# Four slots and a new load order for the raw w_down tiles of the sample's down projection

## The chip, the cores and the metric

One NeuronCore of a Trainium2 chip runs the whole program. The metric is the device time of one execution, in microseconds (us); a profiled execution also has a span, from the first to the last instruction in the trace.

## The reference, cut to what matters

One layer of a hybrid encoder on 1024 prompt frames and 32 sample frames, in float32: RMSNorm, a combined input projection, windowed attention beside a gated mixing group, an output projection with residual, and then the part that this case is about:

```python
def swiglu(h, w_gate, w_up, w_down):
    return (jax.nn.silu(h @ w_gate) * (h @ w_up)) @ w_down      # D_MODEL 1024, D_FF 2816

yp = yp + swiglu(rms_norm(yp, g_ffn[l]), ...)   # 1024 rows
ys = ys + swiglu(rms_norm(ys, g_ffn[l]), ...)   # 32 rows
y = rms_norm(y, g_final)
```

## The kernel before, in words

All matrix products of the prompt are float32 made of three passes over a high and a low part (fp32r), so every operand is first split: ScalarE (ACT) writes the high part, VectorE (DVE) the low part. The FFN is done with a seven-product (Strassen-like) scheme. This case is about the last phase, the down projection (PE from 819 us to the end).

**Stages and groups.** The down projection of the prompt has 7 stages (n = 0 to 6, one product each) of 6 groups (g = 0 to 5). Form k = 6n + g is the pair of operands of group g in stage n: a w part and an x part, 512 KB each (256 KB where g = 5, which has one pair of d_ff tiles in place of two). PE does, for each of 4 token tiles t, 6 matmuls of 128x512 for a group (3 where g = 5), so 24 (12) for a group. The products of stages 0 and 1 are summed in the same four PSUM banks.

**What makes a form.** SP issues all the loads, in the order of its program (`load_w`, `load_x`): load k waits until form k - 3 is split, as there are 3 staging buffers. ACT casts (`down_weight_hi`, `act_hi`, lines 1686 and 1700), DVE subtracts (line 1746), into a ring of 8 forms; form k waits for group k - 8.

**Between stages.** In the first stages, after the casts of the next stage's six forms ACT copies the four finished PSUM tiles out (`copy_out`, line 1716); at n = 0 that is the copy into `down_u`, which bumps `u_copied`. PE's stage 1 adds on to the same banks and waits for that copy tile by tile (`bank_free`). In ACT's program this stands as

```python
for n in range(STAGES - 1):
    for g in range(GROUPS_A_FORM):
        form_hi(n + 1, g)
    if n in (0, 1, 3):
        for t in range(TILES):
            copy_out(n, t)
```

and in PE's `bank_free`, called for every tile of a stage's first group:

```python
elif p == P2:                       # stage 1
    pe.wait_ge(u_copied, t + 1)
```

**The sample.** The 32 sample rows are multiplied with w_down as it is, in plain float32: 22 raw tiles r (11 for each half of d_model, 512 KB each), loaded by `load_raw` (line 806) into slots in the unused `y_acc_odd`. `down_sample(r)` (line 1364) does two matmuls of a tile. `SAMPLE_TURNS` says after which groups (n, g) PE does how many of them; "turn (0,5)" is that after group 5 of stage 0. Tile r goes to slot r % 2 and waits until tile r - 2 has been used (`raw_used`).

**SP's order around it.** Loads 0 to 5, raw tiles 0 and 1, the last stores of the hidden values, loads 6 and 7, `store_sums` (the last 1 MB of `act_sums` to DRAM), then a wait until those have landed (line 838), the sample's residual (line 840), and loads 8, 9, 10, 11. Raw tiles 2 and 3 come behind load 11, tiles 4 and 5 in front of load 14, 6 and 7 in front of load 15, 8 and 9 in front of load 16, 10 in front of load 17.

Of the kernel before, what the change touches and what calls it, by code (L numbers as in the profile page):

```python
# [30 lines left out]
CHUNKS = STEPS // 2  # L31
# [7 lines left out]
P1, P6, P5, P7, P2, P3, P4 = range(PRODUCTS)  # L39
# [29 lines left out]

SAMPLE_BANK = DOWN_B[3]  # L70
QUARTERS = [slice(DEC * x, DEC * x + DEC) for x in range(4)]
SAMPLE_TURNS = {(0, 3): 2, (0, 5): 2, (1, 0): 2, (1, 1): 2, (1, 2): 2, (1, 3): 1,
                (3, 0): 2, (3, 2): 2, (3, 4): 2, (4, 0): 2, (4, 2): 2, (4, 3): 1}
RAW_SLOTS = 2


def raws_before(n, g):

    return sum(c for at, c in SAMPLE_TURNS.items() if at < (n, g))

# [136 lines left out]
def product_count(s, p, j):  # L217

    if isinstance(s, int) and s == 0:
        return PRODUCTS * j + p + 1  # L220
    return 2 * PRODUCTS * s + (2 * p + j + 1)
# [12 lines left out]
def build(nc, a, o):  # L234
# [3 lines left out]
    with ExitStack() as ctx:  # L238
# [3 lines left out]
        def sem(name):  # L242
            return ctx.enter_context(nc.semaphore(name))
# [67 lines left out]
        def place(name, shape, at, dt=F32):  # L311
            return nc.alloc_sbuf_tensor_at(name, shape, dt, offset=at)
# [34 lines left out]
                     place("sample_in_odd", [P, CHUNKS, DEC], h_at + 43008)]  # L347
        y_even = place("y_acc_even", [P, TILES, D], work_at + 40960)
        y_odd = place("y_acc_odd", [P, TILES, D], work_at)
        raw = [y_odd[:, 2 * x:2 * x + 2, 0:512] for x in range(RAW_SLOTS)]  # L350
        y_sample = place("y_acc_sample", [DEC, D], work_at + 57344)
        du = place("down_u", [P, TILES, 512], trans_at)
        resid = [place("resid_0", [P, D], wsp_at), place("resid_1", [P, D], stage_at + 8192)]
# [104 lines left out]
        product_done = sem("product_done")  # L458
# [16 lines left out]
        wd_in_landed = [sem(f"wd_in_landed{x}") for x in range(STAGED_FORMS)]  # L475
        xd_in_landed = [sem(f"xd_in_landed{x}") for x in range(STAGED_FORMS)]
        sample_landed = [sem(f"sample_landed{x}") for x in range(2)]
        raw_landed = [sem(f"raw_landed{x}") for x in range(RAW_SLOTS)]
        raw_used = sem("raw_used")
        sample_back = sem("sample_back")  # L480
        resid_landed = [sem(f"resid_landed{x}") for x in range(2)]
# [84 lines left out]
        def _(sp):  # L566
# [4 lines left out]
            w_down = a["w_down"][0].rearrange("(f p) c -> p f c", p=P)  # L571
# [73 lines left out]
            for n in range(4, UNIT_FFN):  # L645
# [8 lines left out]
                if n in g_state_after:  # L654

                    g = g_state_after[n]
# [61 lines left out]
            def store_sums(c):  # L718

                for j in range(2):  # L720
                    sp.wait_ge(act_sums_ready, 6 * c + (3 * j + 3))
                    sp.dma_start(act_rows[:, bass.ds(STAGES * c + A_S2, 4), 2 * P * j:2 * P * j + 2 * P],
                                 act_sum[j][:, :, :]).then_inc(act_sums_out[j], 16)
# [15 lines left out]
            def store_piece(c, x):  # L739

                sp.wait_ge(t_ready, 4 * PIECES * c + (4 * x + 4))
                sp.dma_start(t_rows[:, bass.ds(c, 1), :, P * x:P * x + P].rearrange("p c x t -> p (c x) t"),
                             t_out[x % 2][:, :, :]).then_inc(t_stored[x % 2], 16)
# [27 lines left out]
            def load_w(k):  # L771

                n, g = divmod(k, GROUPS_A_FORM)
                c0, pairs = GROUP * g, GROUP_PAIRS[g]
                if k >= STAGED_FORMS:
                    sp.wait_ge(w_dn_lo, k - STAGED_FORMS + 1)
                else:
                    sp.wait_ge(product_done, product_count(last, [P1, P1, P5][k], 1))
                if n in PLAIN_OF:
                    e, h = PLAIN_OF[n]  # L780
                    src = w_down[:, 2 * c0 + e:2 * (c0 + pairs):2, 512 * h:512 * h + 512]
                else:
                    src = t_pairs[:, T_OF[n], c0:c0 + pairs, :]
                dst = wd_in[k % STAGED_FORMS][:, 0:pairs, :]
                sp.dma_start(dst, src).then_inc(wd_in_landed[k % STAGED_FORMS], 16)

            def load_x(k):

                m, g = divmod(k, GROUPS_A_FORM)
                c0, pairs = GROUP * g, GROUP_PAIRS[g]  # L790
                if k >= STAGED_FORMS:
                    sp.wait_ge(x_dn_lo, k - STAGED_FORMS + 1)
                else:
                    sp.wait_ge(product_done, product_count(last, [P6, P6, P5][k], 1))
                form = A_OF[STAGE_PRODUCT[m]]
                dst = xd_in[k % STAGED_FORMS][:, 0:pairs, :]
                sp.dma_start(dst, act_pairs[:, form, c0:c0 + pairs, :]).then_inc(xd_in_landed[k % STAGED_FORMS], 16)

            def load_raw(r):

                h, c = divmod(r, CHUNKS)
                if r >= RAW_SLOTS:
                    sp.wait_ge(raw_used, r - RAW_SLOTS + 1)
                else:
                    sp.wait_ge(product_done, product_count(last, P4, 0))
                sp.dma_start(raw[r % RAW_SLOTS], w_down[:, 2 * c:2 * c + 2, 512 * h:512 * h + 512]
                             ).then_inc(raw_landed[r % RAW_SLOTS], 16)

            def load_resid(k):
                if k >= 2:  # L810
                    sp.wait_ge(resid_used, k - 1)
                i = [0, 2, 4, 6, 1, 3, 5, 7][k]
                sp.dma_start(resid[k % 2][:, :], y_scratch[row_tokens(i), :]).then_inc(resid_landed[k % 2], 16)

            last = STEPS - 1
# [8 lines left out]
                    sp.wait_ge(product_done, product_count(last, P7, 1))  # L824
                    sp.dma_start(sample_in[0][:, :, :], sample_scratch.ap()[:, 0, :, :]).then_inc(sample_landed[0], 16)
            store_piece(CHUNKS - 1, 3)
            for r in range(RAW_SLOTS):
                load_raw(r)
            store_step(CHUNKS - 1, 1)
            for j in range(2):  # L830
# [2 lines left out]
            for k in (GROUPS_A_FORM, GROUPS_A_FORM + 1):  # L833
                load_w(k)
                load_x(k)
            store_sums(CHUNKS - 1)
            for j in range(2):
                sp.wait_ge(act_sums_out[j], 16 * CHUNKS)
# [1 line left out]
            sp.dma_start(y_sample[:, :], y_scratch[row_tokens(SAMPLE), :]).then_inc(sample_back, 16)  # L840
            for n in range(1, STAGES):
                for g in range(2 if n == 1 else 0, GROUPS_A_FORM):
                    if g >= 2:
                        for r in range(max(RAW_SLOTS, raws_before(n - 1, g - 2)), raws_before(n - 1, g - 1)):
                            load_raw(r)
                    load_w(GROUPS_A_FORM * n + g)
                    load_x(GROUPS_A_FORM * n + g)
                for r in range(raws_before(n - 1, 4), raws_before(n, 0)):
                    load_raw(r)
                if n in (2, 4, 5):  # L850
                    for k in ((0, 1) if n == 2 else (2, 3) if n == 4 else (4, 5)):
                        load_resid(k)
# [173 lines left out]
        def _(pe):  # L1026
# [326 lines left out]
            def down_sample(r):  # L1353

                h, c = divmod(r, CHUNKS)
                if r == 0:
                    pe.wait_ge(c12_ready, 2 * STEPS)
                    for x in range(2):
                        pe.wait_ge(sample_landed[x], 16)
                if r == CHUNKS:  # L1360
                    pe.wait_ge(u2_down, TILES)
                pe.wait_ge(raw_landed[r % RAW_SLOTS], 16 * (r // RAW_SLOTS + 1))
                for e in range(2):
                    last = mm(ps[QUARTERS[(2 * c + e) % 4], SAMPLE_BANK, :], sample_in[e][:, c, :],  # L1364
                              raw[r % RAW_SLOTS][:, e, :], start=c < 2, stop=c >= CHUNKS - 2)
                last.then_inc(raw_used, 1)

            for n in range(STAGES - 1):
                for g in range(GROUPS_A_FORM):
                    for t in range(TILES):  # L1370
                        down_group(n, g, t)
                    for r in range(raws_before(n, g), raws_before(n, g + 1)):
                        down_sample(r)
# [883 lines left out]
```

## Time and profile before

| what | value |
|---|---|
| three runs | 1063.82, 1065.97, 1066.91 us; median 1065.97 |
| the profiled execution's own time | 1065.66 us |
| its span | 1063.9 us (1.8 us of its time lie outside the span) |
| PE matmul busy | 1022.2 us, 96% of the span |
| DVE, ACT, POOL busy | 625.9, 391.0, 385.3 us |
| DMA in the stretch 841 to 859 us | 308 GB/s, engines 0.87 busy |

The engines: PE is the matmul engine, PEld its weight loads, SPq the queue of DMA issues. A timeline row has the start, the duration, the engine, the line, the operation and the tiles it writes and reads, and in square brackets the idle time before it and what ended that. For a DMA issue the duration is that of the issue, not of the transfer. Consecutive rows of the same kind can be merged: x4 is four of them.

### The profile page before, as it was taken

The page shows a single profiled execution, that of the slowest core. Times are in us where ns is not written, and L with a number is a line of the kernel's source. Part 1 is how long each engine was busy: PE and PEld are TensorE (multiplying, and loading weights), DVE is VectorE, ACT ScalarE, POOL GpSimd, SP SyncE. Part 2 cuts the span into 40 slices and gives each one's busy share as a digit, 9 for nine tenths or more (in the row PEclk, how much of TensorE's full clock was granted, in tenths as well). Part 3 has the DMA queues.
Part 4 walks back from the last instruction along what each step waited for, and adds up shares of the span by engine and source line. Part 5 has one row for each costly group of instructions (what it writes and reads, how often), then busy time and mean ns, then how long its engine had stood idle before and what let it go on. Part 6 is the DMA issues. An engine that isn't in the chain of part 4 may idle for free.

```text
span 1063.9 us, 19541 instructions
## 1 busy us (share of the span) xinstructions
PE 1022.2 (96%) x7160; PEld 934.2 (88%) x7160; DVE 625.9 (59%) x943; ACT 391.0 (37%) x763; POOL 385.3 (36%) x445
## 2 busy tenths in 40 slices
PE   5999999999999699999999999999999969999996
PEld 5999998888887599999999999999999737877785
DVE  5376547665444766666676576567665554454524
ACT  5412144444232433333333333333334354424331
POOL 2010100000000437676686596686762300120045
PEclk9999999999999899999999999999999989999999
DMA  8211331101222434364454544643637898777714
GB/s 282 90 39 42 81 83 43 40 1 64 95 100 90 116 97 147 109 198 133 124 173 123 159 140 125 186 144 110 188 117 261 271 359 293 240 267 254 269 40 163
DMA packets 176258, 155.84 MB, mean 146 GB/s; under 512 B 22352, under 2 KB 143760, under 8 KB 176208
## 3 DMA queue, kind: packets, MB, share of 16 engines
q1 hardware_dynamic: 176208, 155.16, 46.1%
q8 instruction: 33, 0.54, 0.2%
q14 instruction: 17, 0.14, 0.0%
HBM read 114.17 MB, written 41.06 MB: 146 GB/s over the span
## 4 chain that ended last, share of the span: by engine, by line
PE 88%; DVE 4%; DMA 4%; POOL 1%; issue 1%; ACT 1%; SPq 0%; POOLq 0%; ACTq 0%; DVEq 0%
PE ps L1033 27%; PE ps L1034 26%; PE ps L1035 26%; DMA xd_in<-act_scratch 2%; PE ps L1070 1%; PE ps L1364 1%; PE ps L1205 1%; PE ps L1183 1%; DMA act_scratch<-act_sums 1%; DMA out_state_gmlp_v_sample<-work 1%; PE ps L1167 1%; DVE work L1831 1%; DMA y_acc_odd<-in_w_down 1%; DVE ln_st L1825 1%; DMA gain<-in_g_mix 0%
## 5 line engine op out<-in xcount | busy, mean ns | idle before, releaser
L1033 PE MATMUL ps<-x_forms,w_forms 128*128 128x256 f32 (+1 forms) x1232 | 354.0, 287 | 10.5 <-DVE w_forms L1746 8.3
L1034 PE MATMUL ps<-x_forms,w_forms 128*128 128x256 f32 (+1 forms) x1232 | 355.0, 288 | 0.0
L1035 PE MATMUL ps<-x_forms,w_forms 128*128 128x256 f32 (+1 forms) x1232 | 353.6, 287 | 0.0
L1033 PEld LDWEIGHTS ps<-x_forms,w_forms 128*128 128x128 f32 x1232 | 236.3, 192 | 11.2 <-DVE w_forms L1746 5.8
L1035 PEld LDWEIGHTS ps<-x_forms,w_forms 128*128 128x128 f32 x1232 | 236.1, 192 | 0.0
L1034 PEld LDWEIGHTS ps<-x_forms,w_forms 128*128 128x128 f32 x1232 | 235.8, 191 | 0.0
L1033 PE MATMUL ps<-w_dn,x_dn 128*128 128x512 f32 x308 | 121.3, 394 | 0.0
L1035 PE MATMUL ps<-w_dn,x_dn 128*128 128x512 f32 x308 | 119.9, 389 | 0.0
L1034 PE MATMUL ps<-w_dn,x_dn 128*128 128x512 f32 x308 | 119.9, 389 | 0.0
L1746 DVE TENSOR_TENSOR w_forms<-w_sums,w_forms 128x512 fp32r<-128x512 f32 x88 | 74.1, 843 | 68.1 <-ACT w_forms L1570 67.7
L885 POOL TENSOR_SCALAR meansq<-sumsq 128x1 f32<-128x1 f32 (+1 forms) x27 | 10.4, 386 | 256.3 <-ACT xn_ffn L1410 227.0
L1570 ACT CAST w_forms<-w_sums 128x512 fp32r<-128x512 f32 x88 | 54.5, 621 | 131.0 <-PE ps L1035 131.0
L1746 DVE TENSOR_TENSOR w_dn<-wd_in,w_dn 128x1024 fp32r<-128x1024 f32 (+1 forms) x42 | 50.4, 1201 | 86.4 <-ACT w_dn L1686 86.0
L1686 ACT CAST w_dn<-wd_in 128x1024 fp32r<-128x1024 f32 (+1 forms) x42 | 41.1, 978 | 100.9 <-PE ps L1035 69.3
L1033 PEld LDWEIGHTS ps<-w_dn,x_dn 128*128 128x128 f32 x308 | 57.8, 188 | 22.4 <-issue 10.8
L1035 PEld LDWEIGHTS ps<-w_dn,x_dn 128*128 128x128 f32 x308 | 57.8, 188 | 12.2
L1034 PEld LDWEIGHTS ps<-w_dn,x_dn 128*128 128x128 f32 x308 | 57.8, 188 | 11.6
L1746 DVE TENSOR_TENSOR x_dn<-xd_in,x_dn 128x1024 fp32r<-128x1024 f32 (+1 forms) x42 | 50.8, 1209 | 2.3 <-ACT x_dn L1700 1.2
L1746 DVE TENSOR_TENSOR w_forms<-w_stage_even,w_forms 128x512 fp32r<-128x512 f32 x33 | 34.8, 1054 | 25.3 <-ACT w_forms L1570 25.3
L999 POOL TENSOR_TENSOR y_acc_even<-resid,down_u 128x512 f32<-128x512 f32 x4 | 6.3, 1586 | 109.8 <-DVE down_u L2180 90.4
L2062 DVE TENSOR_TENSOR ffn_q<-ffn_q 128x256 f32<-128x256 f32 (+1 forms) x44 | 24.1, 548 | 37.0 <-ACT ffn_q L1589 37.0
L1746 DVE TENSOR_TENSOR w_forms<-w_stage_odd,w_forms 128x512 fp32r<-128x512 f32 x33 | 32.4, 981 | 20.0 <-ACT w_forms L1570 19.8
(234 smaller groups left out, 2071.2 us busy)
## 6 DMA issues: line engine op xcount, KB each, us to landing
xd_in<-act_scratch SPq DMA_DIRECT2D x35, 512.0 KB, 7.1
t_raw<-in_w_down SPq DMA_DIRECT2D x88, 128.0 KB, 2.6
act_scratch<-act_sums SPq DMA_DIRECT2D x22, 512.0 KB, 4.0
y_acc_odd<-in_w_down SPq DMA_DIRECT2D x22, 512.0 KB, 5.6
wd_in<-t_scratch SPq DMA_DIRECT2D x20, 512.0 KB, 7.1
wd_in<-in_w_down SPq DMA_DIRECT2D x15, 512.0 KB, 6.2
stage<-in_w_in SPq DMA_DIRECT2D x28, 256.0 KB, 3.6
w_stage_even<-in_w_gate SPq DMA_DIRECT2D x22, 256.0 KB, 3.4
```

What stands on the lines that cost most here:

```text
L1033: mm(out, wh, xh, start=first, stop=False, skip_group_check=onto)
L1034: mm(out, wh, xl, start=False, stop=False, skip_group_check=onto)
L1035: return mm(out, wl, xh, start=False, stop=last, skip_group_check=onto)
L1070: t = turn(out[:, k, 0:n], src[:, P * k:P * k + P], ident[rows, rows])
L1167: last = mm(out[DH:P, at:at + P], cat[hp, j, odd:odd + DH], k_t[hp, even:even + P], start=True, stop=True)
L1183: t = turn(ps[:, 6, at:at + P], probs[:, u % 3, 2 * h + x, :], ident[:, :])
L1205: last = mm(ps[hc, 7, at:at + DH], v[:, i, hc], probs_t[:, u % 2, 2 * h + x, DH * half:DH * half + DH], start=True, stop=True)
L1364: last = mm(ps[QUARTERS[(2 * c + e) % 4], SAMPLE_BANK, :], sample_in[e][:, c, :], raw[r % RAW_SLOTS][:, e, :], start=c < 2, stop=c >= CHUN ...
L1570: nc.scalar.copy(wf[:, n, 0, :, :], src).then_inc(w_form_hi, 1)
L1686: nc.scalar.copy(w_dn[k % RING][:, 0, 0:pairs, :], wd_in[k % STAGED_FORMS][:, 0:pairs, :]).then_inc(w_dn_hi, 1)
L1746: return nc.vector.tensor_tensor(out, x, hi.bitcast(F32), ALU.subtract)
L2062: nc.vector.tensor_tensor(pq[:, j, 0, 0:w], pq[:, j, 0, 0:w], pq[:, j, 1, 0:w], ALU.add).then_inc(q_ready, 1)
```

## The change

The raw tiles of the first half of d_model (r = 0 to 10) get four slots, one whole tile row of `y_acc_odd` each; the second half keeps two. Every pair has its own place in SP's order: tiles 2 and 3 behind load 7 (in front of `store_sums`), 4 and 5 in front of load 8, 6 and 7 in front of load 11, 8 and 9 in front of load 14, 10 in front of load 16; in the second half 11 and 12 in front of load 23, 13 and 14 in front of 25, 15 and 16 in front of 27, 17 and 18 in front of 30, 19 and 20 in front of 32, 21 in front of 34. PE's turn (1,0) is dropped and those behind it move by one group, to (1,1) to (1,4).

```diff
-SAMPLE_TURNS = {(0, 3): 2, (0, 5): 2, (1, 0): 2, (1, 1): 2, (1, 2): 2, (1, 3): 1,
+SAMPLE_TURNS = {(0, 3): 2, (0, 5): 2, (1, 1): 2, (1, 2): 2, (1, 3): 2, (1, 4): 1,
                 (3, 0): 2, (3, 2): 2, (3, 4): 2, (4, 0): 2, (4, 2): 2, (4, 3): 1}
-RAW_SLOTS = 2
+EARLY_SLOTS, LATE_SLOTS = 4, 2
+
+RAW_LOADS = {(1, 2): range(4, 6), (1, 5): range(6, 8), (2, 2): range(8, 10), (2, 4): range(10, 11),
+             (3, 5): range(11, 13), (4, 1): range(13, 15), (4, 3): range(15, 17), (5, 0): range(17, 19),
+             (5, 2): range(19, 21), (5, 4): range(21, 22)}
+
+def raw_slot(r):
+    return (r % EARLY_SLOTS, r // EARLY_SLOTS + 1) if r < CHUNKS else (
+        EARLY_SLOTS + (r - CHUNKS) % LATE_SLOTS, (r - CHUNKS) // LATE_SLOTS + 1)
...
-        raw = [y_odd[:, 2 * x:2 * x + 2, 0:512] for x in range(RAW_SLOTS)]
+        raw = [y_odd[:, x, :].rearrange("p (e c) -> p e c", e=2) for x in range(EARLY_SLOTS)]
+        raw += [y_odd[:, 2 * x:2 * x + 2, 0:512] for x in range(LATE_SLOTS)]
...
             def load_raw(r):
                 h, c = divmod(r, CHUNKS)
-                if r >= RAW_SLOTS:
-                    sp.wait_ge(raw_used, r - RAW_SLOTS + 1)
+                slot = raw_slot(r)[0]
+                if r < EARLY_SLOTS:
+                    sp.wait_ge(product_done, product_count(last, P4, 0))
+                elif r < CHUNKS:
+                    sp.wait_ge(raw_used, r - EARLY_SLOTS + 1)
                 else:
-                    sp.wait_ge(product_done, product_count(last, P4, 0))
+                    sp.wait_ge(raw_used, max(CHUNKS, r - LATE_SLOTS + 1))
...
             for k in (GROUPS_A_FORM, GROUPS_A_FORM + 1):
                 load_w(k)
                 load_x(k)
+            for r in range(2, EARLY_SLOTS):
+                load_raw(r)
             store_sums(CHUNKS - 1)
...
             for n in range(1, STAGES):
                 for g in range(2 if n == 1 else 0, GROUPS_A_FORM):
-                    if g >= 2:
-                        for r in range(max(RAW_SLOTS, raws_before(n - 1, g - 2)), raws_before(n - 1, g - 1)):
-                            load_raw(r)
+                    for r in RAW_LOADS.get((n, g), ()):
+                        load_raw(r)
                     load_w(GROUPS_A_FORM * n + g)
                     load_x(GROUPS_A_FORM * n + g)
-                for r in range(raws_before(n - 1, 4), raws_before(n, 0)):
-                    load_raw(r)
```

## Rows read from the trace of the kernel before

**Rows 1.** The page: PE's busy time, and the chain that ended last.

```profile
PE 1022.2 (96%) x7160; PEld 934.2 (88%) x7160; DVE 625.9 (59%) x943; ACT 391.0 (37%) x763; POOL 385.3 (36%) x445
...
PE 88%; DVE 4%; DMA 4%; POOL 1%; issue 1%; ACT 1%; SPq 0%; POOLq 0%; ACTq 0%; DVEq 0%
```

**Rows 2.** Waits: engine, line, releaser: us in total, times, longest us.

```profile
PEld ps L1364 <- DMA y_acc_odd<-in_w_down: 11.3, 3, 9.5
...
PE ps L1364 <- DMA y_acc_odd<-in_w_down: 9.1, 1, 9.1
```

**Rows 3.** Timeline of PE around turn (0,5).

```profile
850.28 0.39 PE L1035 MATMUL ps<-w_dn,x_dn 128*128 128x512 f32 x1
859.76 1.06 PE L1364 MATMUL ps<-y_acc_odd,sample_in_even 128*32 128x512 f32 x1 [9.09 <-DMA y_acc_odd<-in_w_down]
...
862.83 0.50 PE L1033 MATMUL ps<-w_dn,x_dn 128*128 128x512 f32 x1
```

**Rows 4.** Timeline of PE around turn (0,3), which waits for nothing.

```profile
840.90 0.39 PE L1035 MATMUL ps<-w_dn,x_dn 128*128 128x512 f32 x1
...
842.21 0.50 PE L1033 MATMUL ps<-w_dn,x_dn 128*128 128x512 f32 x1
```

**Rows 5.** Timeline of PE around turn (1,0).

```profile
868.19 0.39 PE L1035 MATMUL ps<-w_dn,x_dn 128*128 128x512 f32 x1
...
870.25 0.50 PE L1033 MATMUL ps<-w_dn,x_dn 128*128 128x512 f32 x1
```

**Rows 6.** Timeline of SP's issues: the hold behind the sums, load 11, tiles 2 and 3.

```profile
834.42 3.09 SPq L722 DMA_DIRECT2D act_scratch<-act_sums  x2
845.26 0.34 SPq L840 DMA_DIRECT2D y_acc_sample<-y_scratch  x1
845.64 0.43 SPq L785 DMA_DIRECT2D wd_in<-in_w_down  x1
...
853.50 0.34 SPq L797 DMA_DIRECT2D xd_in<-act_scratch  x1
853.88 0.94 SPq L806 DMA_DIRECT2D y_acc_odd<-in_w_down  x2
```

**Rows 7.** Timeline of ACT: casts of forms 8 to 11, the copies, form 12.

```profile
849.33 1.05 ACT L1686 CAST w_dn<-wd_in 128x1024 fp32r<-128x1024 f32 x1 [6.63 <-DMA wd_in<-in_w_down]
...
857.09 1.04 ACT L1700 CAST x_dn<-xd_in 128x1024 fp32r<-128x1024 f32 x1 [0.30 <-DMA xd_in<-act_scratch]
...
858.56 0.61 ACT L1700 CAST x_dn<-xd_in 128x512 fp32r<-128x512 f32 x1
859.08 2.04 ACT L1716 COPY down_u<-ps 128x512 f32<-128x512 f32 x4
862.47 1.05 ACT L1686 CAST w_dn<-wd_in 128x1024 fp32r<-128x1024 f32 x1 [1.35 <-DMA wd_in<-t_scratch]
863.80 1.05 ACT L1700 CAST x_dn<-xd_in 128x1024 fp32r<-128x1024 f32 x1 [0.29 <-DMA xd_in<-act_scratch]
```

**Rows 8.** Windows: start:end, us, PE busy (count), PE's granted clock, DMA share, GB/s.

```profile
856.00:858.00 2.00, 0.00 (x0) 0.50 1.03 369
859.70:861.00 1.30, 1.24 (x4) 0.50 1.05 395
861.00:862.80 1.80, 1.80 (x6) 0.55 1.06 391
862.80:864.00 1.20, 1.20 (x7) 1.00 1.05 387
990.00:1050.00 60.00, 60.00 (x266) 1.00 0.39 137
```

**Rows 9.** Timeline of SP: its issue of raw tiles 15 and 16.

```profile
947.20 0.89 SPq L806 DMA_DIRECT2D y_acc_odd<-in_w_down  x2
```

**Rows 10.** Timeline of ACT: its four copies at n = 3.

```profile
960.20 2.65 ACT L1716 COPY y_acc_odd<-ps 128x512 f32<-128x512 f32 x4 [6.13 <-PE ps L1035]
```

More of the change, by code:

```diff
@@ L477, in build @@
         sample_landed = [sem(f"sample_landed{x}") for x in range(2)]
-        raw_landed = [sem(f"raw_landed{x}") for x in range(RAW_SLOTS)]
+        raw_landed = [sem(f"raw_landed{x}") for x in range(EARLY_SLOTS + LATE_SLOTS)]
         raw_used = sem("raw_used")
@@ L801, in load_raw @@
                 h, c = divmod(r, CHUNKS)
-                if r >= RAW_SLOTS:
-                    sp.wait_ge(raw_used, r - RAW_SLOTS + 1)
-                else:
-                    sp.wait_ge(product_done, product_count(last, P4, 0))
-                sp.dma_start(raw[r % RAW_SLOTS], w_down[:, 2 * c:2 * c + 2, 512 * h:512 * h + 512]
-                             ).then_inc(raw_landed[r % RAW_SLOTS], 16)
+                slot = raw_slot(r)[0]
[3 more added lines that the diff above has]
+                    sp.wait_ge(raw_used, r - EARLY_SLOTS + 1)
+                else:
+                    sp.wait_ge(raw_used, max(CHUNKS, r - LATE_SLOTS + 1))
+                sp.dma_start(raw[slot], w_down[:, 2 * c:2 * c + 2, 512 * h:512 * h + 512]).then_inc(raw_landed[slot], 16)
             def load_resid(k):
@@ L826, in _ @@
             store_piece(CHUNKS - 1, 3)
-            for r in range(RAW_SLOTS):
+            for r in range(2):
                 load_raw(r)
@@ L1361, in down_sample @@
                     pe.wait_ge(u2_down, TILES)
-                pe.wait_ge(raw_landed[r % RAW_SLOTS], 16 * (r // RAW_SLOTS + 1))
+                slot, count = raw_slot(r)
+                pe.wait_ge(raw_landed[slot], 16 * count)
                 for e in range(2):
                     last = mm(ps[QUARTERS[(2 * c + e) % 4], SAMPLE_BANK, :], sample_in[e][:, c, :],
-                              raw[r % RAW_SLOTS][:, e, :], start=c < 2, stop=c >= CHUNKS - 2)
+                              raw[slot][:, e, :], start=c < 2, stop=c >= CHUNKS - 2)
                 last.then_inc(raw_used, 1)
```

## The prediction

> **What bounds the kernel now.** First the page: PE is busy for 96% of the span and makes 88% of the chain that ended last [rows 1], so a change helps only where it lets PE go on sooner. Then the waits: for the raw tiles PE and its weight loads stood 9.1 us in one wait and 11.3 us in three [rows 2]; these are two views of the same gaps and are not added. The timeline shows the gaps. At an ordinary turn the last prompt matmul in front starts at 840.90 and the next at 842.21: 1.31 us [rows 4]. At turn (0,5) the two are 12.55 us apart, 850.28 and 862.83 [rows 3], so 11.24 too many; at turn (1,0) 2.06 us [rows 5], so 0.75 too many. Together 12.0 us, and the change looks as if it could take all of it.
>
> It can't, because of a second wait behind the first. PE's group 6 (stage 1) adds on to the banks of stage 0 and waits for ACT's copies into `down_u`. In ACT's order these copies stand behind the casts of form 11, the last that stage 1 needs. They ran at 859.08 directly behind those casts [rows 7], four in 2.04 us, so the first was done at some 859.6. With the raw tiles there in time, group 6 could have begun at about 859.7 rather than 862.83: 3.1 us is all that this turn has to give while form 11 lands when it does. When load 11 lands is therefore the question.
>
> What sets that landing? SP stood until 845.26 for the landing of the sums that it had stored at 834.42 and later, and only then issued load 8 and on [rows 6]. From there the DMA engines were full (shares of 1.0, 369 to 395 GB/s in the windows from 856 to 864 [rows 8]), and the loads came in the order of issue: ACT takes up a 512 KB part each 1.33 us (862.47 and 863.80 [rows 7]). Load 11's x part was issued at 853.50 and tiles 2 and 3 directly behind it [rows 6]; its cast at 858.56 followed at once on other casts, and the raw tiles came after it (turn (0,5) began at 859.76 [rows 3]).
>
> **The change, part by part.**
>
> *Tiles 2 and 3 in front of the sums.* They are 1 MB. Their slots are free (stage 0 doesn't touch `y_acc_odd`), and SP issues them at about 834.4, 0.94 us of SP's time for two [rows 6], in front of a store that is ready then. The second store waits for POOL anyway. But the store's data stand behind 1 MB more in the queues: 2 x 1.33 = 2.7 us. The sums landed at 845.26, now at about 847.9, and SP waits for exactly that. Ends: 0, if the store's landing is latency and not queue, and 2 x 1.9 = 3.8 us by the slowest spacing that I see (load 8's w part to its x part, 849.33 to 851.16 [rows 7]). I take 2.7, because the queues were backed up from load 6 on.
>
> *Tiles 4 and 5 in front of load 8.* They wait for two used tiles, and turn (0,3) was over at 842.2, so SP doesn't stop. 2.7 us more in front of load 8 and all behind it.
>
> *Tiles 6 and 7 in front of load 11.* They wait for the use of tiles 2 and 3, that is, for turn (0,5), which is now at about 850.6 to 851.6. SP comes there at 852 to 853 and doesn't stop. Load 11 waits for the split of form 8 (its x part cast at about 856.5, DVE behind it, so 859.6), and by then tiles 6 and 7 are in the queue: another 2.7 us for load 11.
>
> *Sum for load 11:* 2.7 + 2.7 + 2.7 = 8.1 us. ACT's casts of it end 8.1 us later, the copies begin at 859.08 + 8.1 = 867.2, the first is done at 867.7, and group 6 begins at 867.75 in place of 862.83: **+4.9 us**. The other three copies follow at 0.5 us each, faster than PE's tiles (6 matmuls of 0.23 us, from 36 matmuls between 842.21 and 850.51 [rows 3, 4]), and cost nothing.
>
> For HBM to SBUF traffic the Trainium skill (DMA: Bandwidth & Descriptors, "Where 436 GB/s comes from") names about 358 GB/s for a core as what binds. The trace disagrees: 387 to 395 GB/s in three of these windows [rows 8], so the measured spacing stands. By the page's figure 512 KB would take an estimated 1.46 us, the six 8.8, and the sum would be 0.7 us more.
>
> *The clock.* Turn (0,5) itself is now done at once. PE then stands from about 851.6 to 867.75. In the kernel before, PE stood from 850.5; its clock was granted at 0.50 at 856 to 858, still without work, stayed there until 862.8 and was 1.00 behind that [rows 8], about 3 us after PE had gone on at 859.76. There the slow stretch fell mostly on the turn's own wait for tile 3. Now it falls on prompt matmuls: 3 us at half speed lose **+1.5 us**. Ends: 0 and 3.0 (6 us of it).
>
> *Turn (1,0) goes.* Its excess goes with it: **-0.75 us**. There are still 6 turns in the first half, each at 1.31 us.
>
> *The moved turns (1,1) to (1,4).* With PE this late, tiles 4 to 7 landed long before. Tiles 8 and 9 wait for turn (1,1), are issued at about 881 and needed by turn (1,3) 12 us later; tile 10 likewise. No stall. DVE's sums of the sample's first half now wait for group 10 in place of 9; group 12's last tile needs them, two group lengths behind. Covered.
>
> *SP's new waits in the second half.* Load 25 now stands behind tiles 13 and 14, which wait for turn (3,0); load 27 behind turn (3,2), 30 behind (3,4), 32 behind (4,0). What is queued behind SP there are loads of forms 25 and on. Forms are split up to 8 ahead of PE, so a hold of up to four groups is covered except at one place: ACT's copies at n = 3 stand behind the casts of form 29. In before's time, SP issues tiles 15 and 16 at 947.20 [rows 9], then loads 27, 28, 29. An idle queue gave its first part 3.7 us behind the issue (845.64 to 849.33 [rows 6, 7]), so 951; then tile 16 and five parts of 512 KB's worth (27, 28, the halves of 29): 951 + 6 x 1.33 = 959, and the copies began at 960.20 [rows 10]. Covered by about 1 us, the thinnest cover in the change; gone, it costs what is missing. Everything else behind shifts with PE: it was busy for all of 990 to 1050 [rows 8].
>
> **Sum:** 4.9 + 1.5 - 0.75 = +5.65 us. On the profiled execution's 1065.66 that is 1071.3; the median of the runs shown stands 0.31 higher, so 1071.6.
>
> **The rivals.**
>
> *A gain that stays hidden in the copies.* If load 11 isn't held back at all (the queues take the raw tiles in parallel, or SP's hold is not lengthened), group 6 begins at 859.7: -3.1, -0.75, and +1.5 for the clock: -2.4 us, 1063.6. Against it: the spacing of 1.33 us at 390 GB/s leaves no room for 3 MB more. 6%, counted with "same".
>
> *Load 11 overtakes.* If a later, smaller load lands by its own time, x 11 comes 4.9 us behind its issue (853.50 to about 858.4) at 859.6: 864.5, group 6 at 865.7: +2.9 + 1.5 - 0.75 = +3.6, 1069.6. The Trainium skill says on the page named above ("Queues, rings and completion order") that completion is not FIFO for an issuing engine, which would permit it. For this there's only the page; the landings here all stood in order. 8%.
>
> *Partly hidden.* The store's landing doesn't move (0 for tiles 2 and 3): +8.1 becomes +5.4, the sum +2.95, 1068.9, at the edge of what can be told from no change. 12%, half of it "same".
>
> *The other side: the wait for the raw tiles was the only one.* If group 6 didn't need the copies, or they ran earlier than I read the order, all of 12.0 us goes: 1054.0. It decides if the copies into `down_u` can be done by 852. For it: PE's wait is put down to the raw tiles alone. Against: the profile names only the last wait, and the copies stand at 859.08 [rows 7]. 5%.
>
> *Worse: the second half too.* If the parts come at 1.9 us rather than 1.33 behind tiles 15 and 16, form 29 is 3.4 us later, past its cover by some 2.4: 1074.0. 9%.
>
> The forecast has 60%. About 0.3%, 3.2 us, is what a measurement of this kernel can tell from no change: faster 0.05, same 0.12 (the first rival and half of the third), slower 0.83. The range: below, the sum without the store's delay and with little of the clock, 1067; above, six parts at 1.9 us (+3.3) and twice the clock's cost (+1.5), 1076.5.
>
> **What would show it.** In the changed kernel's trace: SP's line 840 at about 848 in place of 845.26; turn (0,5) at about 850.6 without a wait; PE's longest wait of the phase in front of group 6, released by ACT's copies into `down_u`, which start at about 867; the first matmuls behind it at a granted clock of 0.5 for some 3 us; no wait on raw tiles at all; group 24 without a wait. I am wrong if group 6 begins before 862, or if it waits for something that isn't the copies.

## The result, and the profile after

The changed kernel takes 1071.26 us (median of four runs, 1070.36 to 1072.49), the kernel before beside it 1065.78 us. The ratio is 1.0057 with a 95% interval of 1.0042 to 1.0072: slower by 5.5 us. The forecast was 1071.6, by a sum of +5.65 us. The profiled execution has a time of 1071.26 us of its own and a span of 1069.5 us, 5.6 us longer than before in both.

First the waits of PE and of its weight loads in the changed kernel, which answer to [rows 2] (engine, line, releaser: us in total, times, longest). Line numbers have moved by some 12: the sample's matmuls are now line 1377, the prompt's 1045 to 1047, ACT's copies 1729.

```profile
PE ps L1045 <- ACT down_u L1729: 16.1, 1, 16.1
...
PEld ps L1045 <- ACT down_u L1729: 17.0, 1, 17.0
```

The waits for raw tiles are gone from the list, all of them. In their place stands one that wasn't there, longer than any before, and ACT ends it. The timeline of PE shows where it is, beside [rows 3]:

```profile
849.82 0.39 PE L1047 MATMUL ps<-w_dn,x_dn 128*128 128x512 f32 x1
850.14 0.62 PE L1377 MATMUL ps<-y_acc_odd,sample_in_even 128*32 128x512 f32 x1
...
867.33 0.80 PE L1045 MATMUL ps<-w_dn,x_dn 128*128 128x512 f32 x1 [16.13 <-ACT down_u L1729]
867.93 0.63 PE L1046 MATMUL ps<-w_dn,x_dn 128*128 128x512 f32 x1
```

Turn (0,5) begins 0.32 us behind the last prompt matmul, as an ordinary turn does, and is over by 851.2. Then nothing until group 6, the first of stage 1. Now ACT, beside [rows 7]: the casts of forms 8 (w and x part) and 10, those of form 11, and the copies that PE waits for.

```profile
855.37 1.04 ACT L1699 CAST w_dn<-wd_in 128x1024 fp32r<-128x1024 f32 x1 [13.22 <-DMA wd_in<-in_w_down]
856.70 1.04 ACT L1713 CAST x_dn<-xd_in 128x1024 fp32r<-128x1024 f32 x1 [0.28 <-DMA xd_in<-act_scratch]
...
862.11 1.04 ACT L1713 CAST x_dn<-xd_in 128x1024 fp32r<-128x1024 f32 x1 [0.31 <-DMA xd_in<-act_scratch]
865.50 0.62 ACT L1699 CAST w_dn<-wd_in 128x512 fp32r<-128x512 f32 x1 [2.34 <-DMA wd_in<-in_w_down]
866.18 0.62 ACT L1713 CAST x_dn<-xd_in 128x512 fp32r<-128x512 f32 x1
866.70 2.04 ACT L1729 COPY down_u<-ps 128x512 f32<-128x512 f32 x4
```

The banks that it copies were finished at about 850. It stood 13.22 us for load 8 and 2.34 us for load 11 (the time of tiles 6 and 7 in the queues) before it came to them. SP's issues, beside [rows 6], show the order that made it so:

```profile
833.23 1.56 SPq L820 DMA_DIRECT2D y_acc_odd<-in_w_down  x2
834.83 2.10 SPq L733 DMA_DIRECT2D act_scratch<-act_sums  x2
847.67 0.34 SPq L855 DMA_DIRECT2D y_acc_sample<-y_scratch  x1
848.06 0.94 SPq L820 DMA_DIRECT2D y_acc_odd<-in_w_down  x2
849.04 0.47 SPq L796 DMA_DIRECT2D wd_in<-in_w_down  x1
...
852.96 1.76 SPq L820 DMA_DIRECT2D y_acc_odd<-in_w_down  x2
857.70 0.35 SPq L796 DMA_DIRECT2D wd_in<-in_w_down  x1
859.03 0.34 SPq L808 DMA_DIRECT2D xd_in<-act_scratch  x1
```

Tiles 2 and 3, the stores of the sums, the hold until 847.67; tiles 4 and 5, loads 8 to 10, tiles 6 and 7, and only then load 11. Last, the windows of PE (start:end, us, PE busy and count, granted clock, DMA share, GB/s), beside [rows 8]:

```profile
853.00:855.00 2.00, 0.00 (x0) 0.84 1.03 383
855.00:864.00 9.00, 0.00 (x0) 0.50 1.05 390
867.00:871.00 4.00, 3.67 (x9) 0.50 0.78 288
871.00:872.00 1.00, 1.00 (x5) 0.78 0.00 0
872.00:874.00 2.00, 2.00 (x11) 1.00 0.00 0
900.00:1056.00 156.00, 156.00 (x700) 1.00 0.60 218
```

The clock fell while PE stood and rose again some 4 us after group 6 had begun; from 900 us on PE is busy without a gap. The DMA engines were full for the whole of the wait.

### The profile page after: what moved, and what is told of

Its sections match the earlier page's. It is cut to its first block, busy times and chain, and to the rows that moved or that the text cites. A ratio compares the mean times of both kernels' runs of the same rounds, so it can differ in the third digit from the quotient of the medians.

```text
span 1069.5 us, 19541 instructions
## 1 busy us (share of the span) xinstructions
PE 1020.1 (95%) x7160; PEld 934.1 (87%) x7160; DVE 627.0 (59%) x943; ACT 391.6 (37%) x763; POOL 386.1 (36%) x445
## 4 chain that ended last, share of the span: by engine, by line
PE 87%; DMA 5%; DVE 4%; POOL 1%; issue 1%; ACT 1%; SPq 0%; POOLq 0%; ACTq 0%; DVEq 0%
PE ps L1045 27%; PE ps L1046 26%; PE ps L1047 26%; DMA xd_in<-act_scratch 2%; PE ps L1082 1%; DMA act_scratch<-act_sums 1%; PE ps L1217 1%; PE ps L1377 1%; PE ps L1195 1%; DMA out_state_gmlp_v_sample<-work 1%; PE ps L1179 1%; DVE work L1844 1%; DVE ln_st L1838 1%; DMA gain<-in_g_mix 0%; DVE work L1855 0%
## 5 line engine op out<-in xcount | busy, mean ns | idle before, releaser
L1045 PE MATMUL ps<-x_forms,w_forms 128*128 128x256 f32 (+1 forms) x1232 | 353.8, 287 | 11.2 <-DVE w_forms L1759 8.6
L1045 PE MATMUL ps<-w_dn,x_dn 128*128 128x512 f32 x308 | 122.1, 396 | 16.1 <-ACT down_u L1729 16.1
L1713 ACT CAST x_dn<-xd_in 128x1024 fp32r<-128x1024 f32 (+1 forms) x42 | 41.1, 978 | 8.7 <-DMA xd_in<-act_scratch 8.4
```

What stands on the lines that cost most here:

```text
L1045: mm(out, wh, xh, start=first, stop=False, skip_group_check=onto)
L1713: nc.scalar.copy(x_dn[k % RING][:, 0, 0:pairs, :], xd_in[k % STAGED_FORMS][:, 0:pairs, :]).then_inc(x_dn_hi, 1)
```

## The experiments

Eight kernels were run, each timed beside the kernel before. What the text says of a profile (a start, a wait, a clock) is read from one profiled execution of each kernel; the times are medians.

**Copies first.** The one edit that the theory stands on: ACT's copies are taken from behind the casts of form 11 to in front of those of form 8, and nothing else is touched.

```diff
                 for g in range(GROUPS_A_FORM):
+                    if n == 0 and g == 2:
+                        for t in range(TILES):
+                            copy_out(n, t)
                     form_hi(n + 1, g)
-                if n in (0, 1, 3):
+                if n in (1, 3):
```

> The changed kernel with ACT's four copies into down_u in front of the casts of form 8 instead of behind those of form 11. Theory (the copies behind form 11 are the new bound): group 6 starts 1.3 us after the last matmul of group 5, near 851.1 instead of 867.33, and the clock stays at 1.00, which takes off 16.2 and about 1.9 us: 1071.3 - 18.1 = 1053.2 us, and up to 1.5 us more where tiles 8 and 9 or tile 10 land within a microsecond of their turns. Rival (load 11 is late for another reason that also holds group 6, such as full DMA queues): at most 3 us faster than the changed kernel, 1068 or more. Rival (the clock falls anyway): about 1055.

Measured: 1054.06 us, ratio to the kernel before 0.9894 (0.9877 to 0.9910). That is 17.2 us below the changed kernel, where 18.1 were expected and the rival allowed 3. ACT's copies and the next cast, and group 6 in PE's timeline:

```profile
847.64 2.62 ACT L1729 COPY down_u<-ps 128x512 f32<-128x512 f32 x4 [5.89 <-PE ps L1047]
854.52 1.05 ACT L1699 CAST w_dn<-wd_in 128x1024 fp32r<-128x1024 f32 x1 [4.25 <-DMA wd_in<-in_w_down]
...
865.45 0.63 ACT L1713 CAST x_dn<-xd_in 128x512 fp32r<-128x512 f32 x1
```

```profile
849.26 0.39 PE L1047 MATMUL ps<-w_dn,x_dn 128*128 128x512 f32 x1
...
850.57 0.50 PE L1045 MATMUL ps<-w_dn,x_dn 128*128 128x512 f32 x1
```

The last matmul of group 5 and the first of group 6 are now 1.31 us apart, an ordinary turn as in [rows 4]. Form 11's x part is cast at 865.45, as late as in the changed kernel, and it harms nothing, as group 11 is far off. So the queues held the copies, not the group. What remains of waits in this phase is 0.6 us of PE for DVE's sums of the sample at group 12, and 0.4 us of its weight loads for a raw tile. The run missed the expected 1053.2 by 0.9 us; that these two waits make up the miss is likely by their size, but not shown.

**The same move in the kernel before.**

> The kernel before with the same move of the copies and nothing else. Theory (two waits side by side, of which the one for tiles 2 and 3 ends last by 3 us): no change, within 0.3% of 1065.8, PE's wait of 9.1 us for the raw tiles at 850 to 860 stays. Rival (the copies were the only bound of group 6 and the waits for the tiles are an artefact of attribution): 3 us or more faster, 1062.7 or less.

Measured: 1066.83 us, ratio 1.0011 (1.0000 to 1.0023): no gain. The wait for tiles 2 and 3 stands as it did in [rows 2], although the copies begin at 847.43 now, in place of 859.08:

```profile
PE ps L1364 <- DMA y_acc_odd<-in_w_down: 9.3, 1, 9.3
```

Alone, the change loses 5.5 us and the move of the copies gains nothing; the two together gain 11 us. Two waits stood side by side in the kernel before, and the list of waits named the one that ended last.

**The ladder of load 11.** Three kernels take the raw tiles out from in front of load 11, pair by pair. First 6 and 7, then 4 and 5 too:

```diff
-RAW_LOADS = {(1, 2): range(4, 6), (1, 5): range(6, 8), ...
+RAW_LOADS = {(1, 2): range(4, 6), (2, 0): range(6, 8), ...      # 6, 7 behind load 11
...
+RAW_LOADS = {(2, 0): range(4, 8), ...                           # 4 to 7 behind load 11
```

> The changed kernel with tiles 6 and 7 loaded behind load 11 instead of in front of it. Theory (the queues serve in order, each tile costs its 1.35 us): load 11 lands 2.7 us sooner, the copies start at 864.0 instead of 866.7, the time is 1071.3 - 2.7 = 1068.6. Rival (the delay is the longer hold of SP alone): no change, 1071.3. Rival (a small load overtakes): no change either, as nothing in front of it counts.

> The changed kernel with tiles 4 to 7 all loaded behind load 11, so only tiles 2 and 3 are in front of it, and in front of the stores of the sums. Theory: load 11 lands 5.4 us sooner, the copies start at 861.3, group 6 at 861.9, the time is 1071.3 - 5.4 = 1065.9, that is no change against the kernel before, although no turn waits for a raw tile. Rival (the delay is the longer hold of SP alone): 1071.3.

And last 2 and 3, the only ones that were also in front of the stores of the sums; turn (0,5) must then become turn (1,0):

```diff
-SAMPLE_TURNS = {(0, 3): 2, (0, 5): 2, (1, 1): 2, ...
+SAMPLE_TURNS = {(0, 3): 2, (1, 0): 2, (1, 1): 2, ...
-RAW_LOADS = {(1, 2): range(4, 6), (1, 5): range(6, 8), ...
+RAW_LOADS = {(2, 0): range(2, 6), (2, 1): range(6, 8), ...
...
-            for r in range(2, EARLY_SLOTS):
-                load_raw(r)
             store_sums(CHUNKS - 1)
```

> The changed kernel with no raw tile in front of load 11 but 0 and 1: tiles 2 to 5 behind load 11, 6 and 7 behind load 12, and turn (0,5) moved to (1,0), so no turn waits. The last step of the ladder of 2.7 us. Theory: the copies start where they did before, at about 858.7, group 6 at 859.3, and the time is 1071.3 - 8.1 = 1063.2, which is all that better slots can give while the copies stand behind form 11 (2.4 us under the kernel before). Rival (tiles 2 and 3 in front of the stores cost nothing, because the stores' landing is latency): as with tiles 4 to 7 behind load 11, 1065.6. Rival (the raw tiles were the only bound): 1054.

Measured, with the start of ACT's copies (timeline of ACT, the row of each; all of them stand directly behind form 11):

| raw tiles in front of load 11 (beside 0 and 1) | time, us | ratio to before | copies start | counted from turn (0,3) |
|---|---|---|---|---|
| 2 to 7 (the changed kernel) | 1071.26 | 1.0057 (1.0042 to 1.0072) | 866.70 | 25.95 |
| 2 to 5 | 1068.37 | 1.0023 (1.0010 to 1.0037) | 864.07 | 23.03 |
| 2, 3 | 1065.62 | 1.0004 (0.9994 to 1.0013) | 860.36 | 20.97 |
| none | 1064.96 | 0.9986 (0.9977 to 0.9995) | 859.26 | 17.55 |
| none, but a wait for 2 and 3 (the kernel before) | 1065.78 | 1 | 859.08 | 17.86 |

```profile
864.07 2.04 ACT L1729 COPY down_u<-ps 128x512 f32<-128x512 f32 x4
```

```profile
860.36 2.04 ACT L1729 COPY down_u<-ps 128x512 f32<-128x512 f32 x4
```

```profile
859.26 2.03 ACT L1727 COPY down_u<-ps 128x512 f32<-128x512 f32 x4
```

The last column takes out that the phase begins up to 2.3 us sooner or later from one execution to the next (turn (0,3) starts at 840.75, 841.04, 839.39, 841.71 and 841.22). In it the pairs cost 2.9, 2.1 and 3.4 us, where 2.7 was put for each. Part of that unevenness is scatter of SP's hold from one execution to the next: counted from the end of the hold (SP's next issue at 847.67, 847.91, 846.67 and 845.76), the copies of the first four rows start 19.0, 16.2, 13.7 and 13.5 us later. So tiles 6 and 7 cost 2.9 us behind the hold, tiles 4 and 5 cost 2.5, and tiles 2 and 3 only 0.2; the last pair acts through the hold itself, which ends 6.4 to 7.3 us behind the start of turn (0,3) in the six kernels that have it in front of the stores, and 4.0 to 4.9 us behind in the four that don't. That a pair behind the load gives its time back refutes both rivals, a hold of SP alone and a small load that overtakes. The kernel with none in front has its copies at the same place of the phase as the kernel before, and no wait for a tile; it is 0.8 us faster by the medians (0.5 to 2.5 us by the interval of the ratio), not the 12.0 of the waits that are gone. It missed its expected 1063.2 by 1.8 us. Two terms were left out of it or too small: turn (0,5), which the changed kernel does while it waits anyway, is on the path once it is turn (1,0) (1.31 us less one matmul of 0.23, so 1.1 us), and the slow clock lasted 5.4 us in place of 4.1 (below; 0.7 us at half speed). Together they are the 1.8 us; neither was tried by itself. The kernel with 2 and 3 in front has no wait for a tile either, and takes the time of the kernel before.

**The slow clock.** This run puts 60 matmuls in front of group 6, in an unused bank; nobody reads their result. They only keep PE at work; the copies stay late. Nothing of the computation is left out.

```diff
+                    if (n, g) == (1, 0):
+                        pe.wait_ge(w_dn_lo, 7)
+                        pe.wait_ge(x_dn_lo, 7)
+                        for c in range(60):
+                            mm(ps[:, DOWN_B[0], :], x_dn[6][:, 0, 0, 0:P], w_dn[6][:, 0, 0, :], start=True, stop=True)
                     for t in range(TILES):
                         down_group(n, g, t)
```

> The changed kernel with 60 matmuls in front of group 6, behind turn (0,5), whose result in an unused bank is never read; the copies stay late. It only keeps PE at work for 13.6 us of the 16.1 us that it would wait. Theory (the slow clock behind the wait costs 3.9 us at half speed, 1.9 us): granted clock 1.00 throughout, group 6 still at about 867.3, the time 1071.3 - 1.9 = 1069.4. Rival (the slow clock costs nothing because something else holds the groups behind): 1071.3.

Measured: 1070.57 us, ratio 1.0050 (1.0036 to 1.0064), 0.7 us under the changed kernel, with intervals that overlap: by the times alone this stays open. The profile is sharper. Group 6 and the windows:

```profile
868.08 0.50 PE L1045 MATMUL ps<-w_dn,x_dn 128*128 128x512 f32 x1 [1.81 <-ACT down_u L1734]
```

```profile
852.00:866.00 14.00, 14.00 (x66) 1.00 1.03 374
868.00:872.00 4.00, 3.92 (x17) 1.00 0.82 301
```

The clock is 1.00 throughout. From the start of group 6 to the end of the span it is 1068.4 - 868.08 = 200.3 us, in the changed kernel 1069.5 - 867.33 = 202.2 us: 1.9 us less, as expected. The span as a whole is only 1.1 us shorter, because the copies came 0.75 us later in this execution (867.45 in place of 866.70), and group 6 with them; the phase had begun 1.2 us later (turn (0,3) at 841.99, not 840.75). So the loss to the slow clock is shown by one profile against one other.

**The second half alone.** The kernel before with only the new order of tiles 11 to 21 (by setting `EARLY_SLOTS` to 2, with the turns and the early order of before):

```diff
-EARLY_SLOTS, LATE_SLOTS = 4, 2
+EARLY_SLOTS, LATE_SLOTS = 2, 2
-RAW_LOADS = {(1, 2): range(4, 6), (1, 5): range(6, 8), (2, 2): range(8, 10), (2, 4): range(10, 11), ...
+RAW_LOADS = {(2, 0): range(2, 4), (2, 2): range(4, 6), (2, 3): range(6, 8), (2, 4): range(8, 10), (2, 5): range(10, 11), ...
```

> The kernel before with the change's order of the loads in the second half alone (tiles 11 to 21); the first half keeps two slots, its turns and its order. Theory (the long holds of SP there are covered by the ring of 8 forms): no change, within 0.3% of the kernel before, no wait of PE between 900 and 1050 us. Rival (the holds make forms 25 to 34 late, or ACT's copies at n = 3 late): 1 to 4 us slower.

Measured: 1066.00 us, ratio 1.0001 (0.9991 to 1.0012): no change. SP does stand there, from load 26 at 939 to tiles 15 and 16 at 948.44, as the prediction had it, and PE doesn't notice:

```profile
900.00:960.00 60.00, 60.00 (x276) 1.00 0.55 197
960.00:1050.00 90.00, 90.00 (x407) 1.00 0.58 214
```

**Copies first, tiles 4 to 7 behind load 11.** Both edits together, to see if the order still matters once the copies don't hang on it.

> The copies in front of the casts of form 8, and tiles 4 to 7 behind load 11. Once the copies don't hang on load 11, its place should not matter. Theory: as with the copies alone, 1054.1, to within 1.5 us (tile 5 lands at about 862.6, turn (1,1) is at about 862). Rival (the order still matters, as the queues are full): 3 us slower or more, through a wait for tile 5 and the slow clock behind it.

Measured: 1054.31 us, ratio 0.9893 (0.9878 to 0.9908), the same as with the copies alone. With the copies first, the place of load 11 is worth nothing either way. These two are the fastest versions found, 1.1% under the kernel before; the one with the copies alone is the smaller edit.

## Why the prediction was right, step by step

- *A second wait behind the first.* Right, and it decides everything. With the copies first the changed kernel gains 17.2 us, and the kernel before nothing.
- *Tiles 2 and 3 in front of the sums, 2.7 us.* SP's line 840 was expected at about 848 and came at 847.67. Counted from turn (0,3), the hold ends 6.92 us behind it where it ended 4.04 before: 2.9 us. With no raw tile there it was 4.05 (845.76 less 841.71). The store waited behind more bytes in the queues (2.7 us), and its landing was not a fixed latency (0), as chosen between the two ends.
- *Tiles 4 to 7, 2 x 2.7 us.* Measured 2.1 and 2.9 (2.5 and 2.9 counted from the end of SP's hold). Together with the first pair the three make 8.4 us by the ladder and 8.1 (25.95 less 17.86) against the kernel before; the sum had 8.1.
- *Group 6 at 867.75, +4.9 us.* It began at 867.33, +4.5, in a phase that began 0.47 us sooner: +5.0 on the phase's own clock.
- *The clock, +1.5 us.* The term was a little small. The 3 us of slow clock of the kernel before became some 4.1 here, so 2.0 us, 1.9 by the experiment. In the two ladder kernels with the earliest group 6 it was longest, 5.4 and 5.7 us.
- *Turn (1,0), -0.75 us.* Behind group 6 the span is 202.2 us where it was 201.1; the clock's 1.9 less 0.75 makes 1.15. It fits the measured 1.1, though it wasn't tried by itself.
- *The total.* On the phase's own clock the terms come to 5.0 + 1.9 - 0.75 = 6.15 us, and the profiled execution began the phase 0.47 us sooner, which leaves 5.7 for a span that grew by 5.6. That the forecast of 5.65 hits the measured 5.5 so closely is in part luck: the clock was put 0.4 us too low, and the start of the phase moves by more than that.
- *The moved turns, and the second half: nothing.* The outcome is right, by the waits and by an experiment. The reading of the thinnest cover, in front of the copies at n = 3, was not. The prediction gave it about 1 us, and said that once it is gone it costs what is missing. In the changed kernel form 29 is cast directly in front of the copies, and they begin 1.02 us behind the start of group 23 (964.84), where it was 0.99 us before (959.21, with [rows 10]). So all of that cover was used up, and it cost nothing:

```profile
964.82 0.62 ACT L1699 CAST w_dn<-wd_in 128x512 fp32r<-128x512 f32 x1
965.34 0.62 ACT L1713 CAST x_dn<-xd_in 128x512 fp32r<-128x512 f32 x1
965.86 2.62 ACT L1729 COPY y_acc_odd<-ps 128x512 f32<-128x512 f32 x4
```

In the kernel with only the late order it was more than used up: the copies begin at 962.16, directly behind form 29 and 1.71 us behind the start of group 23, some 0.7 us late, and PE still has no wait. The prediction had left out that PE needs the copied banks only at group 24, and that starts at 963.31 there, by when the first copy is done (962.16 and 0.6 us):

```profile
962.16 2.04 ACT L1729 COPY y_acc_odd<-ps 128x512 f32<-128x512 f32 x4
...
963.31 0.39 PE L1045 MATMUL ps<-w_dn,x_dn 128*128 128x512 f32 x1
```

The order of the landings bore the whole sum. The Trainium skill says (DMA: Bandwidth & Descriptors, "Queues, rings and completion order") that completion isn't FIFO for an issuing engine. For the time of these loads, with the queues full, order of issue was order of landing as far as ACT's casts and the sample's turns show it; that is no guarantee to build a program on. The Trainium skill's about 358 GB/s for HBM to SBUF (same page, "Where 436 GB/s comes from") was exceeded again, with 383 to 390 GB/s in the windows of the wait.

One thing was missed, in an expectation and not in the prediction: work that lies in a wait is free only as long as the wait is there. Turn (0,5) cost nothing in the changed kernel and 1.1 us when it was moved out of the wait.

## What to carry to other kernels

A list of waits names what came last, and says nothing of what came just before it: ahead of an edit that removes a wait, look up when each other operand and bank of the same instruction was ready, and take the distance to the second as the most that can be had (here 3.1 us of 11.2; the kernel with no raw tile in front of load 11 kept 0.8 of it by the medians). On an engine that works in program order, a copy that frees a bank must not stand behind work that waits for a transfer, unless it needs that transfer. And a prefetch put further forward in one queue of transfers is paid for by every load behind it as long as the queue is full: name the load that someone waits for, and count the bytes in front of it.

## What was not expected of the hardware

The time for which the clock stays at half after PE goes on again differs from one profiled execution to the next: some 3 us in the kernel before, 4.1 in the changed one, 4.0, 5.7 and 5.4 in the three of the ladder (the stretch of matmuls 0.43 us apart). The slow stretch isn't simply longer behind a longer wait of PE: the waits in front were 9.1, 16.1, 13.2, 11.2 and 8.7 us in the same order. What sets its length stays open. In the second of the three:

```profile
860.90:866.70 5.80, 5.71 (x13) 0.50 1.05 388
866.70:868.00 1.30, 1.30 (x7) 0.90 1.05 384
```

It fell after a different time too: 3 us behind PE's last matmul (851.2) in the changed kernel, by the window 853 to 855 above, and 5 us behind it (850.5) in the kernel before, whose windows are

```profile
854.00:855.00 1.00, 0.00 (x0) 1.00 1.06 412
855.00:856.00 1.00, 0.00 (x0) 0.90 1.08 404
```

A term for it needs ends rather than one value: half of the shortest and of the longest stretch seen here, some 1.5 and 2.9 us.
